# Hybrid attention/SSD encoder block: x turned by VectorE's 32-by-32 transposes and block copies, x convolved first

## What is computed

```python
proj = rmsnorm(h, mix_pre_norm) @ w_in          # -> q, k, v, z, xBC, dt, gates
xbc = jax.nn.silu(causal_dwconv(xbc, conv_w, conv_b))      # 4 taps, over tokens
xs, bm, cm = _split(xbc, (SSD_INNER, BC_W, BC_W))          # 2048, 512, 512 channels
xdt = x * dt[..., None]
cb = einsum('bclgn,bcsgn->bgcls', cm, bm)
y_diag = einsum('bgjcls,bcsgjp->bclgjp', cb * lmat, xdt)
states = einsum('bcsgn,bcsgjp->bcgjpn', bm, xdt * decay_states)
y = y_diag + y_off + x * d_skip                 # then gated by silu(z), group-normed
```

## Time and profile before

| what | us |
|---|---|
| median of 3 runs | 1027.19 (1027.01 to 1027.92) |
| the profiled execution, its own time | 1027.51 |
| its span, first to last instruction | 1025.5 |
| TensorE busy in the span | 1014.5 |
| VectorE, ScalarE, GpSimd busy | 626.1, 474.5, 85.4 |
| TensorE clock granted | 1.00 throughout |
| DMA | 111 GB/s mean, 35.8% of 16 engines |

### The profile page before, as it was taken

The page is one execution under the profiler, slowest core; times in us unless marked ns, Lnnn a source line. Parts: engine busy times, 40 slices in busy tenths (PEclk is TensorE's granted clock), DMA queues, the critical chain, the costliest instruction groups (busy, mean ns, idle before and its releaser), DMA issues.

```text
span 1025.5 us, 13506 instructions
## 1 busy us (share of the span) xinstructions
PE 1014.5 (99%) x5199; PEld 844.5 (82%) x5199; DVE 626.1 (61%) x836; ACT 474.5 (46%) x816; POOL 85.4 (8%) x132
## 2 busy tenths in 40 slices
PE   8999999999999999999999999999999999999997
PEld 8888788878888888888888888898888888888886
DVE  5787797888788788444232233676666666632114
ACT  6657757763866577342121232644334334321121
POOL 6003000300120030000000030300000000000001
PEclk9999999999999999999999999999999999999999
DMA  6433551535344332332323435332234233232312
GB/s 195 149 118 94 169 149 52 150 129 144 93 125 134 123 123 83 94 122 82 123 82 109 152 108 161 86 83 82 82 89 115 82 99 105 82 123 82 123 42 82
DMA packets 119226, 113.36 MB, mean 111 GB/s; under 512 B 13999, under 2 KB 108811, under 8 KB 119179
## 3 DMA queue, kind: packets, MB, share of 16 engines
q1 hardware_dynamic: 119179, 112.72, 35.8%
HBM read 109.94 MB, written 2.77 MB: 110 GB/s over the span
## 4 chain that ended last, share of the span: by engine, by line
PE 95%; DMA 1%; ACT 1%; SPq 1%; DVE 1%; issue 0%; POOL 0%; DVEq 0%; POOLq 0%; ACTq 0%
PE ps L1445 22%; PE ps L1447 22%; PE ps L1446 22%; PE ps L1452 5%; PE ps L1454 5%; PE ps L1453 5%; PE ps L1572 3%; PE ps L1641 2%; PE ps L1775 2%; PE ps L1642 2%; PE ps L1643 2%; PE ps L1788 1%; PE ps L1736 1%; PE ps L1608 1%; PE ps L1589 1%; DMA raw<-in_w_up_dram 1%
## 5 line engine op out<-in xcount | busy, mean ns | idle before, releaser
L952 DVE TENSOR_TENSOR wlo<-raw,whi 128x2048 fp32r<-128x2048 f32 (+2 forms) x82 | 184.3, 2248 | 201.5 <-ACT whi L521 201.4
L1445 PE MATMUL ps<-uhi,whi 128*128 128x512 f32 x768 | 301.6, 393 | 0.0
L1447 PE MATMUL ps<-uhi,wlo 128*128 128x512 f32 x768 | 299.1, 389 | 0.0
L1446 PE MATMUL ps<-ulo,whi 128*128 128x512 f32 x768 | 298.9, 389 | 0.0
L521 ACT ACTIVATE whi<-raw 128x2048 fp32r<-128x2048 f32 (+2 forms) x82 | 154.1, 1880 | 168.9 <-PE ps L1454 93.0
L1447 PEld LDWEIGHTS ps<-uhi,wlo 128*128 128x128 f32 x768 | 144.2, 188 | 30.2
L1445 PEld LDWEIGHTS ps<-uhi,whi 128*128 128x128 f32 x768 | 144.2, 188 | 30.0 <-issue 0.8
L1446 PEld LDWEIGHTS ps<-ulo,whi 128*128 128x128 f32 x768 | 144.3, 188 | 29.0
L1377 DVE SCALAR_TENSOR_TENSOR yT<-ps,fpar,yT 128x511 f32<-128x511 f32 x88 | 65.7, 749 | 36.5 <-ACT yT L909 35.0
L909 ACT ACTIVATE yT<-ps,fpar 128x512 f32<-128x512 f32 x44 | 34.1, 779 | 97.8 <-DVE fpar L1372 68.0
L1445 PE MATMUL ps<-rhi,whi 128*128 128x512 f32 x192 | 74.8, 390 | 0.0
(11 more groups left out here) (267 smaller groups left out, 1367.2 us busy)
## 6 DMA issues: line engine op xcount, KB each, us to landing
raw<-in_w_in_dram SPq DMA_DIRECT2D x24, 1024.0 KB
raw<-in_w_up_dram SPq DMA_DIRECT2D x44, 512.0 KB
raw<-in_w_down_dram SPq DMA_DIRECT2D x11, 1024.0 KB
sums_bc<-sum_rows_scratch SPq DMA_DIRECT2D x16, 512.0 KB, 3.8
raw<-in_w_ssd_out_dram SPq DMA_DIRECT2D x8, 1024.0 KB
raw<-in_w_in_dram SPq DMA_DIRECT2D x15, 512.0 KB
grow_bc<-sum_rows_scratch SPq DMA_DIRECT2D x12, 512.0 KB, 5.1
raw<-in_w_attn_out_dram SPq DMA_DIRECT2D x4, 1024.0 KB
```

The lines of the kernel that those rows point to most:

```text
L952: dve.tensor_tensor(wlo[sl][:, 0:width] if into is None else into, raw[sl][:, 0:width], h.bitcast(F32), ALU.subtract).then_inc(s["lo_done" ...
L1445: pe.matmul(bank(b)[:, span], hi_[:, k, c], ah[:, span], start=first and k == ks[0], stop=False)
L1446: pe.matmul(bank(b)[:, span], hi_[:, k, c], al[:, span], start=False, stop=False)
L1447: ins = pe.matmul(bank(b)[:, span], lo_[:, k, c], ah[:, span], start=False, stop=last and k == ks[-1])
```

## The change

- In every group the tiles are convolved in the order x, x, x, x, B, C (it was B, C, x, x, x, x), and SP loads the weight blocks in that order.
- x no longer goes through TensorE and PSUM. VectorE transposes each x tile in 32-by-32 blocks into `zg` (4 instructions of 128x512 per group). The 16 blocks of 32 partitions are put in their place by copies of 32x512: 8 on ScalarE, 8 on GpSimd. None of them begins before the fourth tile is transposed.
- TensorE keeps the turning of B alone (`turn_b`). Its order becomes: z tile 0, `turn_b`, B times C, scores, z tile 1.
- In the start, token tile 2 is scaled on VectorE in place (128x1024) and turned by plain transposes; ScalarE rounds the second q/k/v half after `u_hi(2, 0)`; the head parameters (with a table load) move behind the rounding of block 2.
- Before the up projection, token tile 1 is weighed and rounded in two halves, and TensorE waits for each half; VectorE waits for `h_rstd` before the rest of the second early block.

```diff
 def conv_col(G, f):
-    return G + INNER // P if f == 0 else G + (INNER + STATE_W) // P if f == 1 else G * 4 + f - 2
+    return G * 4 + f if f < 4 else G + (INNER if f == 4 else INNER + STATE_W) // P
+def block_move(i, j):
+    to = x_tok[32 * j:32 * j + 32, :, :].rearrange("p t (f i r) -> p i f t r", f=4, i=4)[:, i]
+    of = zg[32 * i:32 * i + 32, :, :].rearrange("p f (t j r) -> p j f t r", t=NT, j=4)[:, j]
+    return to, of
...
 # GpSimd, group(G), ahead of its other work
+pool.wait_ge(s["blocks_ok"], 4 * (G + 1))
+for i in range(2, 4):
+    for j in range(4):
+        pool.tensor_copy(*block_move(i, j)).then_inc(s["moved_pool"], 1)
...
 # ScalarE, start
-hi(1, 64, None, 4 * QKV0)
 u_hi(0, 1)
 u_hi(1, 1)
 act.activation(xin[:, 3, :], xin[:, 3, :], ACT.Copy, scale=small[:, 11:12])
 u_hi(2, 0)
+hi(1, 64, None, 4 * QKV0)
...
 # ScalarE, group(G)
+def move_x(i, j):
+    act.wait_ge(s["blocks_ok"], 4 * (G + 1))
+    act.activation(*block_move(i, j), ACT.Copy)
 tanh(2)
 hi_next(4)
+act.wait_ge(s["yn_ok"], 4 * G)
 tap(4)
 tanh(3)
+for j in range(3):
+    move_x(0, j)
+act.wait_ge(s["grown"], G * (NT - 1))
 tap(5)
 tanh(4)
-tok(0)
-tok(1)
+move_x(0, 3)
+for j in range(4):
+    move_x(1, j)
+tanh(5)
 skip_x(0)
-tanh(5)
+turned_b()
 gains(0, 0)
 gains(0, 1)
...
     if t == 0:
         tanh_gate(0)
-        for f in range(2, 5):
-            tok(f)
...
 # VectorE, start
-scale_x(2)
 weigh_x(0, 1)
+dve.tensor_scalar(xin[:, 2, :], xin[:, 2, :], small[:, 10:11], None, ALU.mult).then_inc(s["xn"], 1)
...
+lo(1, 2, 4 * QKV0)
 weigh_x(3, 0)
 weigh_x(3, 1)
-lo(1, 2, 4 * QKV0)
...
 # VectorE, group(G)
+def transpose_blocks(f):
+    dve.wait_ge(s["silu_ok"], G * 6 + f + 1)
+    dve.transpose(zg[:, f, :], conv[:, f, :]).then_inc(s["blocks_ok"], 1)
 silu(0)
 lo_next(3)
+transpose_blocks(0)
 if G:
     normalize(G - 1)
 taps(2)
 silu(1)
 taps(3)
+transpose_blocks(1)
 silu(2)
 lo_next(4)
+transpose_blocks(2)
 taps(4)
 silu(3)
+transpose_blocks(3)
 taps(5)
 silu(4)
 silu(5)
...
 # VectorE, times_dt(0)
-dve.wait_ge(s["tok_sb"], G * 5 + 5)
+dve.wait_ge(s["moved_act"], G + 1)
+dve.wait_ge(s["moved_pool"], 8 * (G + 1))
...
 # TensorE, turn_x: matmul with scale_of, else transpose
-if t < NT - 1:
+if t < 2:
...
 # TensorE, group(G), after the six tiles
-tok(0)
-tok(1)
-pe.wait_ge(s["silu_ok"], G * 6 + 2)
+z_tile(0)
+turn_b()
+pe.wait_ge(s["silu_ok"], G * 6 + 6)
 # ... the product of B and C
-z_tile(0)
 # ... scores of t = 0
-if t == 0:
-    for f in range(2, 5):
-        tok(f)
...
 # before the up projection
+weigh_h(1, range(4))                 # VectorE; h_hi(1, ...) on ScalarE alike
+weigh_h(1, range(4, KD))
-weigh_h(1)
```

More of the change, by code:

```diff
@@ L638, in group @@
                     square_y(G - 1)
+                else:
+                    head_parameters()
                 if G == 0:
@@ L845, in hi_of, with h_hi @@
                 hi(n % 2, 64 * (n // 2 + 1), n - 1)
-            def h_hi(t):
-                act.wait_ge(s["h_plain"], t + 1)
-                act.activation(uhi[:, :, t * P:(t + 1) * P], plain(t), ACT.Copy).then_inc(s["h_hi"], 1)
+            def h_hi(t, ks=range(KD)):
+                k = slice(ks[0], ks[-1] + 1)
+                act.wait_ge(s["h_plain"], H_TURNED[t] if ks[-1] == KD - 1 else H_TURNED[t] - 1)
+                act.activation(uhi[:, k, t * P:(t + 1) * P], plain(t)[:, k, :], ACT.Copy).then_inc(s["h_hi"], 1)
             def out_square(t):
@@ L885, in _ @@
             h_hi(0)
-            h_hi(1)
+            h_hi(1, range(4))
+            h_hi(1, range(4, KD))
             out_square(3)
@@ L960, in _ @@
             link(dve.tensor_copy(rtmp[0:NT, 0:P], posi[:, :]))
[L962 to L966, removed]
-            def rest(t, hi_name, done, n=KD):
-                dve.wait_ge(s[hi_name], t + 1)
-                c = slice(t * P, (t + 1) * P)
-                dve.tensor_tensor(ulo[:, 0:n, c], plain(t)[:, 0:n, :], uhi[:, 0:n, c].bitcast(F32), ALU.subtract).then_inc(s[done], 1)
             def scale_x(t):
@@ L1337, in residual, with weigh_h @@
                                          in1=resid[:, t, :], op0=ALU.mult, op1=ALU.add).then_inc(s["d_h"], 1)
-            def weigh_h(t):
-                weigh(t, "hT_mm", par[:, 1, KI:KI + KD], "h_plain")
+            def weigh_h(t, ks=range(KD)):
+                k, n = slice(ks[0], ks[-1] + 1), len(ks)
+                dve.wait_ge(s["hT_mm"], 2 * t + (ks[-1] + 1) // 4)
+                dve.tensor_tensor(plain(t)[:, k, :], two(ps[:, 2 * t:2 * t + 2, :]).rearrange("p (k c) -> p k c", k=KD)[:, k, :],
+                                  par[:, 1, KI + ks[0]:KI + ks[0] + n].unsqueeze(2).to_broadcast([P, n, P]), ALU.mult).then_inc(s["h_plain"], 1)
             def rest_h(t):
-                rest(t, "h_hi", "h_ok")
+                c = slice(t * P, (t + 1) * P)
+                dve.wait_ge(s["h_hi"], H_TURNED[t])
+                dve.tensor_tensor(ulo[:, :, c], plain(t), uhi[:, :, c].bitcast(F32), ALU.subtract).then_inc(s["h_ok"], 1)
             for t in range(2):
@@ L1347, in _ @@
                 residual(t)
+            dve.wait_ge(s["h_rstd"], 1)
             lo(1, N_E + 2, h=ahead_hi[1], into=ahead_lo[1])
@@ L1625, in norm_sums @@
                 for t in range(NT):
-                    ins = pe.matmul(ps[32 * t:32 * t + 32, 7, 0:P], ones[:, 0:32], conv[:, 2, t * P:(t + 1) * P], start=True, stop=True)
+                    ins = pe.matmul(ps[32 * t:32 * t + 32, 7, 0:P], ones[:, 0:32], conv[:, 0, t * P:(t + 1) * P], start=True, stop=True)
                 ins.then_inc(s["norm_mm"], 1)
@@ L1923, in _ @@
             pe.wait_ge(s["lo_done"], N_E + 1)
-            pe.wait_ge(s["h_hi"], NT // 2)
-            rests_last(half[0], ahead[0], NT // 2)
+            rests_last(half[0], ahead[0], NT // 2, H_TURNED[1] - 1, H_TURNED[1])
             turn_h(2)
@@ L1930, in _ @@
             features(3, 1, 1, u, span=half[0], split=ahead[1])
-            pe.wait_ge(s["h_hi"], NT)
-            gates, values = rests_last(half[1], ahead[0], NT)
+            gates, values = rests_last(half[1], ahead[0], NT, H_TURNED[3], H_TURNED[3])
             gates.then_inc(s["up_mm"], 1)
```

120 lines of the change are left out of this document (61 added, 59 removed).

## The result

The changed kernel takes 1033.16 us (median of 6 runs, 1030.29 to 1034.06), the kernel before 1027.38 us (6 runs) on the same chip: ratio 1.0048, 95% interval 1.0035 to 1.0061. It is slower by 5.8 us. The prediction was 1028.1 us with a range of 1019.5 to 1035.0, slower being the likeliest of its three signs by little (0.36).

What follows compares the result with a forecast made beforehand. TensorE, busy 1014.5 of 1025.5 us, was taken as the bound. Groups +3.75, start -2.3, up projection -0.5 gave +0.95 on the profiled 1027.51; with the median 0.3 lower, 1028.1 us, range 1019.5 to 1035.

Steps and rivals of the forecast that it cites:

- the forecast's own: Main case, chance 0.5: in the groups `pT` ends late by ScalarE's list; time between 1025.3 and 1030 us.
- slow transposes: Rival, chance 0.17: VectorE's block transposes in the groups take up to 1.2 us each; +7.5 us, 1035.6 us.
- late GpSimd copies: Rival, chance 0.08: GpSimd's shifted copies cost over 1.8 us each, delaying `xdt` and the state product; 1045 us or more.
- Step 1: TensorE's list: 64 x transposes leave the groups, 6.98 us, and tile 2's start saves 0.87; -7.85 us if nothing else moved.
- Step 2: Group 1, VectorE: transposes at 0.62 us each; last block ready at 163.6, TensorE ending the sixth tile at 163.76.
- Step 3: Groups, ScalarE up to `pT`: eight copies at 0.60 us add 4.8 us, `pT` ends late; +0.7 us a group.
- Step 4: Group 0: no idle time hides the first VectorE transpose, so blocks come 0.95 us later; +1.65 us.
- step 5: Start: reordered roundings fill ScalarE's DMA wait, shortening TensorE's wait for `uhi`, and tile 2 saves transposes; -2.3 us.
- step 6: Before the up projection: with rounding in halves TensorE can start half a rounding sooner; -0.5 us (-0.2 to -0.8).
- the saving stays: Rival, chance 0.25: in the groups the engines absorb the copies and ScalarE's list does not end last; about 1020 us.

Runs made afterwards that it cites:

- experiment 2: Changed kernel with only ScalarE's eight block copies reordered: last tap and tanh 4 first, three copies, tanh 5, then five copies; 1029.31 us.
- experiment 6: Changed kernel with half-length copies, ScalarE's share placed in its idle times, and the gains ahead of the copy of turned B; 1018.20 us.
- experiment 1: Changed kernel with extra unused matmuls of ones filling TensorE's waits for the fifth and sixth silus in every group; 1031.37 us.
- experiments 3 to 6: Changed kernel with GpSimd making twelve copies; making all; half-length copies shared by idle time; those plus gains first: 1026.82, 1023.58, 1021.44, 1018.20 us.
- e_order: The kernel of experiment 2: changed kernel with only ScalarE's eight block copies in another order; 1029.31 us.
- e_x_only: Changed kernel with the start, head parameters' exponential and part before the up projection as before; only the turning of x is new; 1033.65 us.

## Why the prediction was near, and 5 us too low

1033.16 us lies in the whole range (1019.5 to 1035.0) but outside the forecast's own, 1025.3 to 1030. The upper end of the whole range was drawn for slow transposes and late GpSimd copies, and neither came. What carried the time there was mostly the clock, 4.2 us, for which the prediction has no term. So the sign and the place of the first loss were foreseen; that the range still held the time is luck in part.

**Step 1** held in number: 64 transposes and 8 doubled records left TensorE (5199 to 5127 instructions). That its busy time would fall by 8 us, which I had named as the sign of it, did not come. Where the clock holds, it does: 6.5 us less in experiment 2, 7.9 in experiment 6.

**Step 2** held in groups 1 to 3. A transpose takes 0.71 us with its tail and keeps the pace of 0.62 that I took. The last one ends at 166.62, 0.15 us before the last matmul of tile 6 does (166.77), and I had 163.6 and 163.76. The slow-transpose rival falls.

**Step 3** had the mechanism: all eight copies fall on ScalarE's list, and `pT` ends late. Predicted +0.7 us a group; where the clock stayed at 1.00 it was +0.99 (group 1), and +1.05 with the waits filled. The term that was too small is the copy, 0.64 us instead of 0.60, 5.12 us for eight; the rest of ScalarE's list took 13.0 us for my 13.1. The +0.95 that I gave for 0.63 is what came. The bounds had it in them. How the waiting was shared out I had less well: before the product of B and C 1.32 us for 1, plus 0.35 before the turning of B, and at `pT` 0.45 us in group 1 and none in TensorE's rows of the others, for some 1.5. The Trainium skill (ScalarE: Activation LUTs, What ACT_TABLE_LOAD costs) states 186 ns plus 0.833 ns per element, an estimate of 0.61 us by that page; the rows show 0.63 for one. Its overlap of back-to-back ones does not appear: three took 1.92 us and five 3.20. I had kept that rule out of the sum, rightly.

I put VectorE beside GpSimd at nothing, with up to 0.6 us for each silu. The fifth took 0.88 us instead of 0.68 beside GpSimd's copies, the last, which comes after them, 0.69. With twelve copies on GpSimd the two took 1.88 together. The price is there, but small, and leaving it out of the sum was right: VectorE stood idle for 1.28 us between the two silus, so the slow fifth one bears on the 0.35 us before the turning of B alone, and the 1.6 us that I gave for the wait before B times C did not come.

**Step 4** is where the prediction was furthest off: "blocks 0.95 later, so +1.65 us". Group 0 cost +5.10. For a kernel with the old start the step is near: without the parts outside the groups the blocks are ready 0.79 us behind the end of tile 6, and group 0 costs +1.77. With them they are ready at 70.45, 1.85 us behind it. TensorE comes there 3.70 us earlier than without them, VectorE's blocks only 2.64. I had added up VectorE's new links but not taken off what step 5 gives TensorE. Without the clock's fall group 0 would cost +2.93 (20.18).

**The step that is missing is the clock.** I read it as 1.00 throughout and never asked what new waits would do to it; in the kernel before, 1.70 and 1.26 us of waiting had left it there. Against the filled waits it cost 2.17 us in group 0, 1.14 in group 2 and 0.93 in group 3, together 4.2 us of the groups' +10.25, in the profiled execution; in some of the others it fell less. Taking the groups' +6.0 without it, instead of +3.75, leaves 2.3 us to steps 3 and 4: group 0 1.3, the others 3 x 0.35.

**Step 5** was right (-2.07 for -2.3; the wait for `uhi` is 0.22 us, and another of 0.6 came, for tile 2 scaled by VectorE, that I had as hidden or 0.3), **step 6** too low (-1.6 for -0.5): the wait of 1.26 us went altogether, and so did the 0.26 before the turning of h. How much of it comes depends on when a block of the up weights lands, as experiment 1 showed. But steps 5 and 6 were added to the groups as if independent, and they are not: in this kernel they brought 0.5 us of 3.2.

Of the rivals, "the saving stays" is false of this kernel, and true of the turning itself: experiments 3 to 6 show the saving come back as ScalarE's list is relieved, whole in the last of them. I had held against it that no block is ready in ScalarE's idle 4.15 us before tap 5; that is true of the fourth tile and not of the first two. GpSimd's copies took 0.66 us each for my 1.0 and ended at 171.96, 7.5 us before `xdt` (179.43); it could have been given more.

## What to carry to other kernels

When work leaves the engine that bounds a kernel for one that was just keeping pace, look where the receiving engine idles and cut the work so that it fits there; the same blocks moved made a group 18.3 or 16.7 us long, only by the place and the engine of the copies. Anchor each engine's list to its own past: an edit that brings one engine forward may bring the others forward by less (here TensorE by 3.7 us, VectorE's blocks by 2.6), and the rest of the gain turns into waiting. And price a new wait on TensorE by what its clock may do behind it, not by its length alone.

## What the runs showed of the hardware that I had not expected

- Short waits can halve TensorE's clock, and the same waits need not. In the changed kernel 2.18 and 1.32 us, 2 us apart, were followed by a clock of 0.67 and then 0.50 in group 0; 0.35 and 1.32 us left it at 1.00 in group 1 and were followed by a fall in groups 2 and 3. 2.06 us in the start were followed by a fall, 1.70 in the kernel before were not. Over all the kernels here, behind the first matmul, the clock fell at the end of each wait of 2.06 to 2.38 us or soon behind it (five waits, in five kernels). It stayed at 1.00 behind the pairs of 1.65 and 1.22 us in e_order and of 1.15 and 1.30 us in e_x_only, both in group 0. What decides was not settled here. It spreads the times of the kernel: the lowest of its six runs (1030.29 us) had a mean clock of 0.998, the profiled one (1034.03) 0.992.
- A GpSimd copy of 32x256 takes 0.53 us beside 0.66 for 32x512, so most of it did not depend on the length between these two. The eight of 32x512 took 5.28 us in the changed kernel and 6.08 in experiment 2, where they lie beside VectorE's last taps and silus. ScalarE's take 0.42 and 0.64 (four in 1.69, five in 3.20).
- Partition-shifted copies of 32 partitions on ScalarE follow one another without overlap, as the earlier trace rows had shown for reads from PSUM (three in 1.92 us, eight in 4.81).
